# A decoder layer on one core: the conditioning matrix read in a first third and then by slices inside the token chunks

## The chip, the cores and the metric

The kernel runs on one core of a Trainium2 chip. The metric is the device time of one launch in microseconds, the median of several runs; lower is better.

## The reference, cut to what matters

One layer works on 2048 prompt tokens and 64 sample tokens (8 sequences of 8). A conditioning vector per sequence (one for the prompt, eight for the samples, so nine rows) is multiplied by a matrix of 1024 x 6144 and gives six modulation vectors of 1024 each:

```python
mod = c @ w_ada + b_ada
sh1, sc1, g1, sh2, sc2, g2 = jnp.split(mod, 6, axis=-1)
u = x * (1.0 + sc1[:, None]) + sh1[:, None]
proj = u @ w_in
...
mix = jnp.concatenate([y_pool, y_lru], axis=-1) @ w_out
x = _layer_norm(ALPHA * x + (1.0 + g1[:, None]) * mix, ln1_g, ln1_b)
u2 = x * (1.0 + sc2[:, None]) + sh2[:, None]
y_moe = _hier_moe(u2, w_group, b_group, w_route, b_route, w_gate, w_up, w_down)
x = _layer_norm(ALPHA * x + (1.0 + g2[:, None]) * y_moe, ln2_g, ln2_b)
```

Only the first third of `mod` (sh1 and sc1) is needed before the projection `proj`. The other four vectors are first used after the output projection `mix`. Between them stand the two mixers: a pooling mixer with windows of 2, 4, 8 and 16 tokens, and a recurrence with a four-tap convolution, two gates and a scan along the tokens. All numbers are 32-bit floats.

## The kernel before, in words

Each engine has its program written out by hand, in order, and waits on counting semaphores; nothing reorders it. The constants KD = 8 (blocks of 128 rows of a 1024-row matrix), NG = 4 (blocks of 128 channels of a mixer) and NCH = 8 (chunks of C = 256 prompt tokens) count the loops.

The start. SyncE (SP) issues all loads: the conditioning rows, three pieces of the matrix w_ada (each 1024 x 512, 2 MiB), small vectors, states, sample rows, then w_in in four parts of 1.5 MiB, and between these the nine other pieces of w_ada (L296 to L317), each when TensorE (PE) is done with the buffer it goes to. PE multiplies each piece by the turned conditioning rows `cT`, eight products of 128 x 512 per piece (L1463). VectorE (DVE) adds the bias (L985), adds 1 where a scale or a gate stands (L988, L989), and PE turns the first third into `modT`. SP stores the other two thirds to HBM (`mod_d`, L328). PE then turns the states and the sample rows, multiplies the modulated sample rows by w_in (24 products, L1554), and the sample tokens go through both mixers as chunk 0. ScalarE (ACT) and GpSimd (POOL) meanwhile split w_in into a high and a low part, with DVE.

The chunks. A chunk of 256 tokens is `mixers(i)` on PE: twelve column blocks ("orders" 0 to 11) of the projection, each of 24 products, which `project` writes to two PSUM banks in turn, with the gates' products ahead of orders 8 and 9 and the pooling products behind orders 9 to 11; then `turn_chunk(i + 1)` turns the next tokens. Orders 0 to 3 feed the convolution, 4 to 7 the pooling, 8 to 11 the recurrence's output gate. On DVE a trip of the loop, `chunk(i)`, is: the four pooling groups of chunk i, the guard, the low part of the next chunk's turned tokens (`u_low(i + 1)`), the recurrence of groups 0 to 2 of chunk i, the convolution of chunk i + 1 (`conv_chunk(i + 1)`, which needs orders 0 to 3 of that chunk), and the recurrence of group 3 of chunk i. So a trip on DVE ends in the middle of the next chunk on PE.

Behind the chunks. SP loads w_out in eight blocks (L355), the first four after the store of chunk 7's output, the rest after 17 small stores of sample states; ACT splits w_out (L726) when all eight are there.

Of the kernel before, what the change touches and what calls it, by code (L numbers as in the profile page):

```python
# [5 lines left out]
P = 128  # L6
# [78 lines left out]
def build(nc, A):  # L85
    with ExitStack() as ctx:
# [38 lines left out]
        def part_at(off, *shape):  # L125
# [27 lines left out]
        w_ada = [place(ada_arena, 10240 + n * 4096, KD, 512) for n in range(3)]  # L153
        mod = place(ada_arena, 22528, 6 * D)
# [55 lines left out]
        cT = sb("cT", [P, KD, NM])  # L210
# [36 lines left out]
            consts c_in vec_in ba_in gates_in gates_zero wpool_in st_in x_loaded xs_loaded w_in_in ada0 ada1 ada2  # L247
            cT_mm cT_ok ada_mm ada_ok mod_ok modT_mm modT_ok vec_mm vec_ok st_mm xsT_mm mod_stored dve_order act_order
# [9 lines left out]

        block = ctx.enter_context(nc.Block())
# [3 lines left out]
        ada_d = A["w_ada"][0].rearrange("(k p) (g n) -> g p k n", p=P, n=512)  # L263
# [30 lines left out]
        def _(sp):  # L294

            sp.dma_start(c_rows[0:1, :], A["c_prompt"]).then_inc(S["c_in"], 16)  # L296
            sp.dma_start(c_rows[1:NM, :], A["c_sample"]).then_inc(S["c_in"], 16)
            for n in range(3):
                sp.dma_start(w_ada[n], ada_d[n]).then_inc(S[f"ada{n}"], 16)
            sp.dma_start(mod[0:NM, :], all_parts(A["b_ada"][0], NM)).then_inc(S["ba_in"], 16)  # L300
            for r, name in enumerate(("b_conv", "b_a", "b_x", "lru_lambda", "pool_scale")):
                sp.dma_start(row_v[r:r + 1, :], A[name]).then_inc(S["vec_in"], 16)
            sp.dma_start(row_v[V_WCONV:NV, :], A["w_conv"][0]).then_inc(S["vec_in"], 16)
            sp.dma_start(row_a[0:DEC_B * PB, :], A["state_pool"][0].rearrange("b t c -> (b t) c")).then_inc(S["st_in"], 16)
            sp.dma_start(row_b[0:DEC_B * CB, :], A["state_conv"][0].rearrange("b t c -> (b t) c")).then_inc(S["st_in"], 16)
            sp.dma_start(row_c[0:DEC_B, :], A["state_lru"][0]).then_inc(S["st_in"], 16)
# [4 lines left out]
            sp.dma_start(w_in[:, 0:2, :], w_in_d[:, 0:2, :]).then_inc(S["w_in_in"], 16)  # L311
            with sp.Fori(1, 4) as j:
                sp.wait_ge(S["w_in_in"], 16 * j)
                sp.dma_start(w_in[:, ds(2 * j, 2), :], w_in_d[:, ds(2 * j, 2), :]).then_inc(S["w_in_in"], 16)
                for n in range(3):
                    sp.wait_ge(S["ada_mm"], 3 * j + n - 2)
                    sp.dma_start(w_ada[n], ada_d[ds(3 * j + n, 1)].rearrange("a p k n -> p (a k) n")).then_inc(S[f"ada{n}"], 16)  # L317
            sp.dma_start(xin, xp_d[0]).then_inc(S["x_loaded"], 16)
            sp.wait_ge(S["gates_zero"], 1)
# [7 lines left out]
            sp.wait_ge(S["mod_ok"], 1)  # L327
            sp.dma_start(mod_d[:, 2 * D:6 * D], mod[0:NM, 2 * D:6 * D]).then_inc(S["mod_stored"], 16)  # L328
# [15 lines left out]
            sp.wait_ge(S["ylru_ready"], NG)  # L344
            sp.dma_start(yT_d[NT - 1][:, :, 0:NS], yT[:, :, 0:NS]).then_inc(S["y_stored"], 16)
            with sp.Fori(1, NCH) as i:
                load_x(i + 1)
                store_y(i)

# [7 lines left out]
            sp.wait_ge(S["out_evac"], 3)  # L357
            load_out((2, 3, 4, 7))
# [10 lines left out]
            def load_rows():  # L369

                sp.wait_ge(S["wout_lo_dve"], KD - OUT_POOL)
                sp.wait_ge(S["mod_stored"], 16)
# [133 lines left out]
        def _(pool):  # L506
# [25 lines left out]
            for k in range(KD // 2):  # L532
                pool.wait_ge(S["win_hi"], k + 1)
                pool.wait_ge(S["ada_mm"], 10 + min(k, 1))
                pool.tensor_tensor(w_in_lo[:, k, :], w_in[:, k, :], w_in_hi[:, k, :].bitcast(F32),
                                   ALU.subtract).then_inc(S["win_lo_pool"], 1)
# [137 lines left out]
        def _(act):  # L674
            o = Order(act, S["act_order"])

            act.wait_ge(S["vec_ok"], 1)
# [4 lines left out]
            for k in range(KD):  # L682
                act.wait_ge(S["w_in_in"], 16 * (k // 2 + 1))
                if k == 6:
                    act.wait_ge(S["ada_mm"], 10)
                act.activation(w_in_hi[:, k, :], w_in[:, k, :], ACT.Copy).then_inc(S["win_hi"], 1)
# [262 lines left out]
        def _(dve):  # L949
            o = Order(dve, S["dve_order"])  # L950

            dve.wait_ge(S["cT_mm"], 1)
            dve.tensor_copy(cT[:], bank[6][:, 0:KD * NM].rearrange("p (k r) -> p k r", r=NM)).then_inc(S["cT_ok"], 1)
# [26 lines left out]
            dve.wait_ge(S["ba_in"], 16)  # L980
            with dve.Fori(0, 4) as j:
                for n in range(3):
                    dve.wait_ge(S["ada_mm"], 3 * j + n + 1)
                    cols = mod[0:NM, ds(1536 * j + 512 * n, 512)]
                    dve.tensor_tensor(cols, bank[n][0:NM, :], cols, ALU.add).then_inc(S["ada_ok"], 1)  # L985
            dve.wait_ge(S["ada_ok"], 12)

            o.step(dve.tensor_scalar(mod[0:NM, SC1:SH2], mod[0:NM, SC1:SH2], 1.0, None, ALU.add))  # L988
            dve.tensor_scalar(mod[0:NM, SC2:6 * D], mod[0:NM, SC2:6 * D], 1.0, None, ALU.add).then_inc(S["mod_ok"], 1)  # L989
# [790 lines left out]
```

## Time and profile before

| what | us |
|---|---|
| median of 3 runs | 1458.19 |
| lowest and highest run | 1457.39, 1458.48 |
| the profiled execution, first to last instruction (span) | 1455.0 |
| the profiled execution's own time | not in the profile apart from its span |
| PE busy | 1251.6 (86%) |
| DVE busy | 890.4 (61%) |
| ACT busy | 516.9 (36%) |
| POOL busy | 419.3 (29%) |

The mean granted clock of TensorE is 0.924 of its full 2.4 GHz. Busy time of PE counts pipelined products, so a busy PE isn't PE at its peak. The median of the runs lies 3.2 us above the span. The slices of the page show the DMA engines busy in the first hundred microseconds and nearly idle during the chunks, which take PE from 158.7 us to 514 us.

### The profile page before, as it was taken

To read this page: it belongs to the slowest core of one execution; us is meant where nothing else is said; L and a number is where in the kernel's file an instruction comes from. 1 tells how busy PE (TensorE), PEld (TensorE's weight loads), DVE (VectorE), ACT (ScalarE), POOL (GpSimd) and SP (SyncE) were. 2 spreads that over 40 slices of the span, in tenths; PEclk is the share of its full clock that TensorE was granted. 3 is DMA by queue.
4 is the path that set the end of the run, shared out by engine and by line. 5 is a ranking of instruction groups with operands and counts; after the bars stand their busy time and mean duration, and the time that the engine had idled before them with its cause. 6 is when DMAs were issued, how large, how long until landed. Compare 5 with 4: busy or idle time off the path is not lost.

```text
span 1455.0 us, 23155 instructions
## 1 busy us (share of the span) xinstructions
PE 1251.6 (86%) x6575; PEld 975.4 (67%) x6576; DVE 890.4 (61%) x1751; ACT 516.9 (36%) x907; POOL 419.3 (29%) x438
## 2 busy tenths in 40 slices
PE   6798899999998955999997169999999999985664
PEld 1113899999997944888885048888888888872221
DVE  2013868998988676556555845456664654224886
ACT  1100455544455331222221134445544534222331
POOL 1030122221122245565653311111111111106882
PEclk9898899999999977999997569999999999996896
DMA  8970101110111253343443266757867683316883
GB/s 276 387 272 4 37 1 58 58 58 3 54 58 58 93 190 126 132 153 139 159 133 113 79 231 221 263 210 257 278 229 238 241 277 115 115 77 235 293 291 113
DMA packets 112334, 230.17 MB, mean 158 GB/s; under 512 B 11381, under 2 KB 61049, under 8 KB 112277
## 3 DMA queue, kind: packets, MB, share of 16 engines
q1 hardware_dynamic: 93711, 162.15, 33.3%
q0 software_dynamic: 11680, 42.47, 8.5%
q10 hardware_dynamic: 6912, 25.17, 4.3%
q8 instruction: 15, 0.25, 0.1%
q14 instruction: 16, 0.13, 0.0%
HBM read 169.62 MB, written 60.27 MB: 158 GB/s over the span
## 4 chain that ended last, share of the span: by engine, by line
PE 69%; DVE 16%; DMA 4%; issue 4%; ACT 4%; SPq 2%; POOL 1%; POOLq 0%; DVEq 0%; ACTq 0%
PE bank L1489 18%; PE bank L1491 17%; PE bank L1490 17%; PE bank L1436 6%; PE bank L1463 4%; DVE arena L1400 2%; PE bank L1554 2%; DVE st L1165 1%; DVE arena L1159 1%; PE bank L1510 1%; DVE arena L1409 1%; PE bank L1624 1%; DMA arena<-in_w_in 1%; DVE parts L1092 1%; PE bank L1740 1%
## 5 line engine op out<-in xcount | busy, mean ns | idle before, releaser
L1489 PE MATMUL bank<-parts 128*128 128x256 f32 (+2 forms) x1616 | 569.1, 352 | 25.3 <-POOL parts L571 17.6
L1491 PE MATMUL bank<-parts 128*128 128x256 f32 (+2 forms) x1616 | 552.6, 342 | 0.0
L1490 PE MATMUL bank<-parts 128*128 128x256 f32 (+2 forms) x1616 | 552.0, 342 | 0.0
L1489 PEld LDWEIGHTS bank<-parts 128*128 128x128 f32 x1616 | 308.6, 191 | 63.4 <-POOL parts L571 18.0
L1491 PEld LDWEIGHTS bank<-parts 128*128 128x128 f32 x1616 | 308.1, 191 | 35.8
L1490 PEld LDWEIGHTS bank<-parts 128*128 128x128 f32 x1616 | 309.0, 191 | 31.9
L1436 PE MATMUL bank<-ident,arena 128*128 128x128 f32 (+4 forms) x788 | 118.0, 282 | 26.3 <-DMA arena<-u_d,tok_now 10.4
L1436 PEld LDWEIGHTS bank<-ident,arena 128*128 128x128 f32 (+4 forms) x788 | 94.7, 146 | 53.5 <-issue 15.8
L1740 PE MATMUL bank<-arena 128*128 128x512 f32 (+1 forms) x136 | 80.3, 748 | 50.9 <-ACT arena L925 39.6
L1331 DVE TENSOR_TENSOR parts<-arena,parts x90 | 104.9, 1221 | 17.9 <-ACT parts L859 14.2
L620 POOL COPY tok_now<-tok_i 128x1 int32 (+1 forms) x48 | 9.4, 195 | 364.7 <-PE bank L1436 347.9
L1343 DVE TENSOR_TENSOR arena<-arena,bank 128x256 f32<-128x256 f32 x48 | 20.2, 421 | 142.7 <-ACT arena L869 142.0
L549 POOL TENSOR_TENSOR arena<-arena 128x256 f32<-128x256 f32 (+1 forms) x36 | 26.1, 728 | 270.1 <-DVE h_last L1098 247.3
L1463 PE MATMUL bank<-ada_arena,cT 128*9 128x512 f32 x192 | 85.6, 608 | 16.2 <-DMA ada_arena<-in_w_ada 16.2
L1740 PEld LDWEIGHTS bank<-arena 128*128 128x128 f32 (+1 forms) x136 | 30.3, 233 | 99.6 <-issue 62.8
L859 ACT ACTIVATE parts<-arena x90 | 88.7, 1052 | 0.2 <-issue 0.2
L869 ACT ACTIVATE arena<-bank 128x256 f32<-128x256 f32 x48 | 18.5, 385 | 178.7 <-PE bank L1491 178.7
L707 ACT ACTIVATE arena<-bank,proj_b 128x256 f32<-128x256 f32 x64 | 30.4, 475 | 142.0 <-PE bank L1491 142.0
L1155 DVE TENSOR_TENSOR arena<-bank,arena 128x512 f32<-128x512 f32 (+1 forms) x34 | 21.8, 684 | 84.7 <-PE bank L1491 84.7
L1463 PEld LDWEIGHTS bank<-ada_arena,cT 128*9 128x9 f32 x192 | 17.5, 93 | 82.5 <-issue 82.5
L589 POOL TENSOR_TENSOR arena<-arena 128x1024 f32<-128x1024 f32 (+1 forms) x17 | 56.4, 3318 | 55.4 <-ACT arena L808 55.4
L1338 DVE TENSOR_TENSOR parts<-bank,parts 128x512 fp32r<-128x512 f32 x96 | 61.9, 686 | 16.6 <-ACT parts L864 16.5
(226 smaller groups left out, 1640.4 us busy)
## 6 DMA issues: line engine op xcount, KB each, us to landing
ada_arena<-in_w_ada SPq DMA_DIRECT2D x12, 2048.0 KB, 11.4
ys_d<-arena ACTq DMA_DIRECT2D x48, 512.0 KB
arena<-in_w_gate SPq DMA_DIRECT2D x16, 1024.0 KB, 6.1
arena<-in_w_up SPq DMA_DIRECT2D x16, 1024.0 KB, 9.8
arena<-in_w_down SPq DMA_DIRECT2D x16, 1024.0 KB, 14.1
arena<-in_x_prompt SPq DMA_DIRECT2D x8, 1024.0 KB, 6.7
yT_d<-arena SPq DMA_DIRECT2D x16, 512.0 KB, 4.4
arena<-yT_d SPq DMA_DIRECT2D x16, 512.0 KB, 4.8
```

Of the source, the lines that this page charges most:

```text
L589: o.step(pool.tensor_tensor(x1[b][0:n, :], z[b][0:n, :], row_tiles[0:n, 1, :], ALU.mult))
L707: act.activation(dst, bank[2 + m % 2][:, 0:C], ACT.Identity, bias=proj_b[:, m:m + 1]).then_inc(S["proj_evac"], 1)
L859: act.activation(part(w_hi, e & 1, n), raw_part(e & 1, n), ACT.Copy).then_inc(S["w_hi"], 1)
L1331: dve.tensor_tensor(part(w_lo, e & 1, n), raw_part(e & 1, n), part(w_hi, e & 1, n).bitcast(F32), ALU.subtract).then_inc(S["w_lo"], 1)
L1338: dve.tensor_tensor(xT_lo[:, k, :], bank[h][:, :].rearrange("p (k n) -> p k n", n=P), xT_hi[:, k, :].bitcast(F32), ALU.subtract).then_inc( ...
L1400: dve.scalar_tensor_tensor(z2[b][0:n, :], xo[b][0:n, :], ALPHA, z2[b][0:n, :], ALU.mult, ALU.add).then_inc(S["comb_used"], 1)
L1436: return pe.transpose(out, in_, ident[0:rows, 0:rows])
L1463: last = pe.matmul(bank[n][0:NM, :], cT[:, k, :], w_ada[n][:, k, :], start=k == 0, stop=k == KD - 1)
L1489: pe.matmul(out, x_hi, w_hi, start=start, stop=False)
L1490: pe.matmul(out, x_hi, w_lo, start=False, stop=False)
L1491: return pe.matmul(out, x_lo, w_hi, start=False, stop=stop)
L1740: last = pe.matmul(bank[2 * b + h][0:n, :], dg[b][0:n, k, 0:n], rows[0:n, 512 * h:512 * h + 512], start=k == 0, stop=k == 1)
```

## The change

Of w_ada only the first 2048 columns are read and multiplied ahead: eight loads of 1 MiB, one for each block of 128 rows, and for each block four products whose outputs go to PSUM partitions 0, 32, 64 and 96 of one bank. The other 4096 columns go by blocks of 128 rows as well: block 0 after the sample rows' projection, block k = 1 to 7 in chunk k, in two halves ("slices") of 2048 columns, four products each, ahead of orders 4 and 5. DVE adds each slice to a sum in SBUF (`mod_out`); it picks the chunk's columns of `cT` into `cT_now` at the head of its trip. The bias of these columns is added in chunk 8, and eight stores bring the sum to `mod_d` ahead of the loads of w_out. The small loads go to ACT's queue. The products of the sample rows with w_in run block by block, each behind its part of the load.

```diff
-        w_ada = [place(ada_arena, 10240 + n * 4096, KD, 512) for n in range(3)]
-        mod = place(ada_arena, 22528, 6 * D)
+        w_ada = [place(ada_arena, 12288 + k * 2048, 2048) for k in range(KD)]
+        w_ada0 = place(ada_arena, 24576, 2, 2048)
+        w_ada_next = [at(2048, 2048), at(5184, 2048)]
+        mod_in = at(3072, 512)
+        mod_out = at(8768, 2, 512)
+        b_out = at(2048, 2, 512)
...
+            for k in range(KD):
+                sp.dma_start(w_ada[k], ada_d[k][:, 0:2048]).then_inc(ada_in[k], 16)
             sp.dma_start(xs[0:NS, :], xs_d).then_inc(S["xs_loaded"], 16)
+            for j in range(4):
+                sp.dma_start(w_in[:, 2 * j:2 * j + 2, :], w_in_d[:, 2 * j:2 * j + 2, :]).then_inc(S[f"w_in{j}"], 16)
+            sp.wait_ge(S["cT_mm"], 1)
             sp.dma_start(xin, xp_d[0]).then_inc(S["x_loaded"], 16)
+            sp.wait_ge(S["ada_mm"], KD)
+            sp.dma_start(w_ada0, ada_d[0][:, 2048:6144].rearrange("p (b n) -> p b n", b=2)).then_inc(S["ada0_in"], 16)
...
+            sp.wait_ge(S["prj_copied"], 1)
+            load_slice(1, 0)
+            load_slice(1, 1)
             sp.dma_start(yT_d[NT - 1][:, :, 0:NS], yT[:, :, 0:NS]).then_inc(S["y_stored"], 16)
-            with sp.Fori(1, NCH) as i:
+            with sp.Fori(1, NCH - 1) as i:
                 load_x(i + 1)
+                for b in range(2):
+                    sp.wait_ge(S["slice_mm"], 2 * i + 1 + b)
+                    load_slice(i + 1, b)
                 store_y(i)
+            load_x(NCH)
...
+            store_y(NCH - 1)
+            sp.wait_ge(S["slice_ok"], 2 * KD + 1)
+            for b in range(2):
+                for j in range(4):
+                    cols = slice(2048 * b + 512 * j + 2048, 2048 * b + 512 * j + 2560)
+                    sp.dma_start(mod_d[:, cols], mod_out[32 * j:32 * j + NM, b, :]).then_inc(S["mod_stored"], 16)
...
             sp.wait_ge(S["out_evac"], 3)
+            sp.wait_ge(S["mod_stored"], 16 * 8)
             load_out((2, 3, 4, 7))
...
+            def add_slice(n, b, src):
+
+                dve.wait_ge(S["slice_ok"], n)
+                dve.wait_ge(S["slice_mm"], n + 1)
+                dve.tensor_tensor(mod_out[:, b, :], src[:, :], mod_out[:, b, :], ALU.add).then_inc(S["slice_ok"], 1)
...
+            dve.wait_ge(S["slice_mm"], 2)
+            o.did(dve.tensor_scalar(mod_out[0:64, 0, :], bank[1][0:64, :], 1.0, None, ALU.add))
+            o.step(dve.tensor_copy(mod_out[64:P, 0, :], bank[1][64:P, :]))
+            dve.tensor_scalar(mod_out[:, 1, :], bank[0][:, :], 1.0, None, ALU.add).then_inc(S["slice_ok"], 2)
...
             def chunk(i, last=False):
 
+                if not last:
+                    dve.wait_ge(S["slice_ok"], 2 * i)
+                    dve.tensor_copy(cT_now[:], cT[:, ds(i, 1), :].rearrange("p a r -> p (a r)")).then_inc(S["cT_picked"], 1)
+                if last:
+                    dve.wait_ge(S["bias_in"], 16 * 8)
+                    dve.wait_ge(S["slice_ok"], 2 * KD)
+                    dve.tensor_tensor(mod_out, mod_out, b_out, ALU.add).then_inc(S["slice_ok"], 1)
+                for b in range(0 if last else 2):
+                    add_slice(2 * i + b, b, bank[4 + b])
                 for g, w in enumerate(WINDOWS):
...
+            for k in range(KD):
+                if k == 4:
+                    turn_vectors()
+                pe.wait_ge(ada_in[k], 16)
+                for j in range(4):
+                    last = pe.matmul(bank[0][32 * j:32 * j + 32, :], cT[:, k, :], w_ada[k][:, 512 * j:512 * j + 512],
+                                     start=k == 0, stop=k == KD - 1)
+                last.then_inc(S["ada_mm"], 1)
+
+            def ada_slice(c, w, out):
+
+                for j in range(4):
+                    last = pe.matmul(out[32 * j:32 * j + 32, :], c, w[:, 512 * j:512 * j + 512], start=True, stop=True)
+                last.then_inc(S["slice_mm"], 1)
...
-            def mixers(i, turn_next):
+            def mixers(i, turn_next, slices=False):
                 for order in range(3 * NG):
+                    if slices and order in (4, 5):
+                        b = order - 4
+                        pe.wait_ge(S["gates_evac"], 2 * NG * i)
+                        pe.wait_ge(S["cT_picked"], i)
+                        pe.wait_ge(S[f"ada_in{b}"], 16 * i)
+                        ada_slice(cT_now[:], w_ada_next[b], bank[4 + b])
+                    if slices and order == 2 * NG:
+                        pe.wait_ge(S["slice_ok"], 2 * i + 2)
```

On PE, in the loop over chunks, between order 3 and order 5 (the L1523 to L1525 products are those of `project`, in the numbering of the changed kernel; L1503 is `ada_slice`):

```order
L1525 MATMUL bank<-parts 128x256
L1561 REGISTER_ALU
L1563 REGISTER_ALU [waits cT_picked,gates_evac]
L1503 MATMUL bank<-arena,cT_now 32x512 [waits ada_in0]
L1503 MATMUL bank<-arena,cT_now 32x512 x3
L1571 REGISTER_ALU
L1523 MATMUL bank<-parts 128x256 [waits proj_evac]
```

Before, the products of order 4 followed those of order 3 with only the wait on `proj_evac` between; now a wait on `cT_picked` and four slice products stand ahead of them, and everything behind is queued behind that wait.

On DVE, at the head of a trip of the loop over chunks, the kernel before (the L1063 copy is the last of `conv_chunk(1)`, L1073 the first pooling sum):

```order
L1063 COPY arena<-arena 128x3 [waits xc_ready]
L1142 UNCONDITIONAL_BRANCH
L1142 ISA
L1073 TENSOR_TENSOR arena<-arena 128x256 [waits proj_evac]
L68 ISA
```

and the changed kernel at the same place:

```order
L1092 COPY arena<-arena 128x3 [waits xc_ready]
L1180 UNCONDITIONAL_BRANCH
L1180 ISA
L1097 ISA [waits slice_ok]
L1097 COPY cT_now<-cT 128x32
L1018 REGISTER_ALU [waits slice_ok]
L1019 TENSOR_TENSOR arena<-bank,arena 128x512 [waits slice_mm]
L1018 REGISTER_ALU [waits slice_ok]
L1019 TENSOR_TENSOR arena<-bank,arena 128x512 [waits slice_mm]
L1106 ISA
L1111 TENSOR_TENSOR arena<-arena 128x256 [waits proj_evac]
```

The copy into `cT_now` is the trip's first instruction, behind the whole of the trip before, and two sums that wait for the slices now stand ahead of the pooling.

On SP, behind the chunks, the changed kernel (L331 stores chunk 7's output, L363 the modulation, L370 loads w_out):

```order
L331 DMA yT_d<-arena 1024x1x128 [waits ylru_ready,pool_evac]
L331 DMA yT_d<-arena 1024x1x128
L363 DMA mod_d<-arena 9x512 [waits slice_ok]
L363 DMA mod_d<-arena 9x512 x7
L370 DMA arena<-in_w_out 128x1024 [waits mod_stored,out_evac]
L370 DMA arena<-in_w_out 128x1024 x3
```

Before, the first load of w_out followed the store directly; now eight stores and the wait for their landing stand between.

## Rows read from the trace of the kernel before

**Rows 1.** Page, chain of work that ended last: shares of the span by engine

```profile
PE 69%; DVE 16%; DMA 4%; issue 4%; ACT 4%; SPq 2%; POOL 1%; POOLq 0%; DVEq 0%; ACTq 0%
```

**Rows 2.** Windows: stretch, length, busy by engine (instructions), clock, DMA share, GB/s

```profile
60.00:80.00 20.00, 20.00 (x48) 4.22 (x47) 1.44 (x4) 1.76 (x2) 0.00 (x0) 1.00 1.03 386
```

**Rows 3.** Timeline of PE, the start: start, us, line, operation [idle before <- releaser]

```profile
9.72 15.30 PE L1463 MATMUL bank<-ada_arena,cT 128*9 128x512 f32 x32 [4.97 <-DMA ada_arena<-in_w_ada]
...
44.03 63.28 PE L1463 MATMUL bank<-ada_arena,cT 128*9 128x512 f32 x144 [11.22 <-DMA ada_arena<-in_w_ada]
113.14 1.87 PE L1436 MATMUL bank<-ident,ada_arena 9*128 9x9 f32 x16 [5.83 <-DVE ada_arena L989]
...
120.72 23.02 PE L1554 MATMUL bank<-arena 128*65 128x512 f32 x48 [1.86 <-DVE arena L1007]
...
155.17 3.69 PE L1436 MATMUL bank<-ident,arena 128*128 128x128 f32 x16
158.68 0.58 PE L1489 MATMUL bank<-parts 128*128 128x256 f32 x1
```

**Rows 4.** Timeline of DVE, the start

```profile
107.46 0.68 DVE L985 TENSOR_TENSOR ada_arena<-bank,ada_arena 9x512 f32 x1 [6.19 <-PE bank L1463]
108.17 3.67 DVE L988 TENSOR_SCALAR ada_arena<-ada_arena 9x2048 f32<-9x2048 f32 x1
...
145.06 0.11 DVE L1021 MEMSET arena<- 128x60 f32 x1 [17.82 <-PE bank L1436]
```

**Rows 5.** Timeline of SP's queue, the start: issues of loads

```profile
0.82 0.35 SPq L296 DMA_DIRECT2D arena<-in_c_prompt  x1
...
1.57 4.46 SPq L299 DMA_DIRECT2D ada_arena<-in_w_ada  x3
```

**Rows 6.** Chain of work in order of time: first product of chunks 2 and 3

```profile
202.65 0.38 PE bank L1489
...
246.25 0.38 PE bank L1489
```

**Rows 7.** Timeline of ACT: evacuation of order 3 in chunks 1 and 2

```profile
170.78 0.47 ACT L707 ACTIVATE arena<-bank,proj_b 128x256 f32<-128x256 f32 x1 [2.33 <-PE bank L1491]
...
214.45 0.47 ACT L707 ACTIVATE arena<-bank,proj_b 128x256 f32<-128x256 f32 x1 [2.33 <-PE bank L1491]
```

**Rows 8.** Timeline of DVE: chunk 1's first pooling sum; the recurrence during chunk 2

```profile
179.61 0.43 DVE L1073 TENSOR_TENSOR arena<-arena 128x256 f32<-128x256 f32 x1
...
204.70 0.29 DVE L1051 TENSOR_SCALAR arena<-arena 128x256 f32<-128x256 f32 x1 [1.20 <-ACT arena L747]
...
225.82 0.28 DVE L1051 TENSOR_SCALAR arena<-arena 128x256 f32<-128x256 f32 x1
...
229.83 0.15 DVE L1098 COPY h_last<-arena 128x1 f32<-128x1 f32 x1
```

**Rows 9.** Source line L1463: count, ns min/median/max, first and last start

```profile
L1463 PE MATMUL bank<-ada_arena,cT x192: 592/592/1061, 9.7 to 106.7; 128*9 128x512 f32 x192
```

**Rows 10.** Timeline of PE at its restart behind the chunks

```profile
531.69 0.79 PE L1489 MATMUL bank<-parts 128*128 128x512 f32 x1 [17.56 <-POOL parts L571]
```

**Rows 11.** Windows there (columns as in Rows 2)

```profile
532.00:534.00 2.00, 2.00 (x6) 1.52 (x6) 2.00 (x2) 0.00 (x0) 2.00 (x1) 0.50 0.10 37
534.00:536.00 2.00, 2.00 (x9) 1.59 (x8) 1.97 (x2) 0.00 (x0) 1.00 (x1) 0.79 0.83 277
```

**Rows 12.** Timeline of SP's queue behind the chunks

```profile
495.04 3.53 SPq L355 DMA_DIRECT2D arena<-in_w_out  x4
...
504.06 0.28 SPq L362 DMA_DIRECT2D result<-arena  x1
504.38 0.28 SPq L363 DMA_DIRECT2D result<-arena  x1
508.64 1.79 SPq L355 DMA_DIRECT2D arena<-in_w_out  x4
```

**Rows 13.** Timeline of ACT behind the chunks: the split of w_out

```profile
516.92 7.68 ACT L726 ACTIVATE parts<-arena 128x1024 fp32r<-128x1024 f32 x8 [2.27 <-DMA arena<-in_w_out]
```

More of the change, by code:

```diff
@@ L209, in build @@
         ones = sb("ones", [P, P])
[L210 removed]
+        cT = sb("cT", [P, KD, 32])
+        cT_now = sb("cT_now", [P, 32])
         modT = sb("modT", [P, 2 * KD, NM])
@@ L257, in build @@
             fsd_ready fnorm fg_ok fo_ok os0 os1""".split()}
+        ada_in = [sem(f"ada_k{k}") for k in range(KD)]
         block = ctx.enter_context(nc.Block())
@@ L1451, in _ @@
             pe.wait_ge(S["cT_ok"], 1)
-            def ada(j, first=False):
-                for n in range(3):
-                    if first and n == 2:
-                        turn_vectors()
-                    pe.wait_ge(S[f"ada{n}"], 16 * (j + 1))
-                    if not first:
-                        pe.wait_ge(S["ada_ok"], 3 * j + n - 2)
-                    for k in range(KD):
-                        last = pe.matmul(bank[n][0:NM, :], cT[:, k, :], w_ada[n][:, k, :], start=k == 0, stop=k == KD - 1)
-                    last.then_inc(S["ada_mm"], 1)
-            ada(0, first=True)
-            with pe.Fori(1, 4) as j:
-                ada(j)
+            for k in range(KD):
+                if k == 4:
+                    turn_vectors()
+                pe.wait_ge(ada_in[k], 16)
+                for j in range(4):
+                    last = pe.matmul(bank[0][32 * j:32 * j + 32, :], cT[:, k, :], w_ada[k][:, 512 * j:512 * j + 512],
+                                     start=k == 0, stop=k == KD - 1)
+                last.then_inc(S["ada_mm"], 1)
+            def ada_slice(c, w, out):
+                for j in range(4):
+                    last = pe.matmul(out[32 * j:32 * j + 32, :], c, w[:, 512 * j:512 * j + 512], start=True, stop=True)
+                last.then_inc(S["slice_mm"], 1)
             pe.wait_ge(S["mod_ok"], 1)
-            for k in range(2 * KD):
-                last = turn(bank[6][:, k * NM:(k + 1) * NM], mod[0:NM, k * P:(k + 1) * P], NM)
+            for i in range(4):
+                last = turn(bank[6][:, i * P:(i + 1) * P], mod_in[:, i * P:(i + 1) * P], P)
             last.then_inc(S["modT_mm"], 1)
@@ L1550, in _ @@
             pe.wait_ge(S["uTs_ready"], 1)
-            for n in range(3):
-                cols = slice(DH, 2 * DH) if n == 0 else slice(0, DH) if n == 1 else slice(2 * DH, 3 * DH)
-                for k in range(KD):
+            for k in range(KD):
+                if k % 2 == 0:
+                    pe.wait_ge(S[f"w_in{k // 2}"], 16)
+                for n in range(3):
+                    cols = slice(DH, 2 * DH) if n == 0 else slice(0, DH) if n == 1 else slice(2 * DH, 3 * DH)
                     last = pe.matmul(bank[2 + n][0:NS + 1, :], uTs[:, k, :], w_in[:, k, cols], start=k == 0, stop=k == KD - 1)
-                last.then_inc(S["rows_mm"], 1)
+                    if k == KD - 1:
+                        last.then_inc(S["rows_mm"], 1)
             for n in range(3):
```

84 lines of the change are left out of this document (38 added, 46 removed).

## The prediction, made before the changed kernel ran

> **What bounds the kernel now.** The chain of work that ended last comes first: 69% of the span is PE [rows 1], so a change is worth what it does to PE's own sequence, stage by stage. Two stages matter here. In the start, the timeline of PE shows what it does until the first chunk's first product at 158.68 us: the products with w_ada begin at 9.72 and, after an 11.22 us wait for a load, run from 44.03 for 63.28 us [rows 3]. In the windows the loads move 386 GB/s meanwhile [rows 2], so this stage is bound by loads and PE together, and nothing of chunk 1 can go on beside it. In the chunks PE is the bound, at 246.25 - 202.65 = 43.60 us per chunk [rows 6], and DVE lags behind it: the timeline of DVE is what the reader has to hold against PE's.
>
> **The start, part by part.** A product with a 512-column piece costs 63.28 / 72 = 0.88 us, since each leaves two records [rows 3, 9].
>
> Loads: of w_ada 8 MiB instead of 24 come first. The first 2 MiB took from 1.57 to 9.72 [rows 3, 5]; at 386 GB/s that is 5.4 us of moving and 2.7 of lead. With SP's first issue at 0.82 [rows 5], 1 MiB every 2.7 us lands its first part at 6.2 and its last at 0.8 + 2.7 + 8 x 2.7 = 25.2.
>
> What four products into four partition strips cost (one slice, s) no row shows. Bounds: four one after another, 4 x 0.88 = 3.52; all at once, 0.88. Each product is two records, and the second reuses the first one's strip; if only neighbours overlap, the four take five half-products, 5 x 0.44 = **2.2 us**. I take that, which is also the middle. The Trainium skill, "TensorE: Matmul & The Clock Gate", Part 3, says that products with outputs at different 32-partition strips run concurrently, with 2.38 times the speed for three, and that they start and end in order. By 2.38 the four would take some 1.5 us (an estimate from that page), and the sum below would be some 12 us lower; no run here shows it.
>
> Last product: 25.2 + 2.2 = 27.4. Then one sum of 0.68 [rows 4] in place of the 5.7 us from 107.46 to 113.14 [rows 3, 4]: 28.3 with handoffs. From 113.14 to 120.72 takes 7.58, of which 1.87 are 16 small turns; four turns of 128x128 take 3.69 / 4 = 0.92 instead [rows 3]: 34.9. The 24 sample products take 23.02 [rows 3]: 57.9. Their loads (6.5 MB behind 25.2, so 42) are there in time by blocks. From 143.74 to 158.68 is 14.94 [rows 3], which stays, and ahead of the stage that DVE begins at 145.06 [rows 4] now stand two slices (4.4) and three sums of 0.68: 6.4. Chunk 1 starts at 57.9 + 14.9 + 6.4 = **79.2, a gain of 79.5**. With s = 0.88 the gain is 83.4; with 3.52 PE and not the loads sets the first part (6.2 + 8 x 3.52 = 34.4) and it is 70.
>
> The small loads on ACT's queue I cost at nothing: the first product's piece lands at 6.2, and ACT has nothing to do before w_in. If the conditioning rows came late behind the big loads, each microsecond would show one for one.
>
> **The chunks.** PE now waits at order 4 for DVE to pick the columns, which DVE does at the head of its trip [the order listings]. Where does that head lie? In chunk 2, PE starts at 202.65 [rows 6] and is done with order 3 when ACT evacuates it, 214.45 [rows 7]. DVE starts the recurrence at 204.70 and ends group 3 at 229.98 [rows 8]; between, its timeline has no gap of note, so it is behind with work, not waiting. With 0.2 us for the copy the pick comes at 230.2: PE **waits 15.7 us** in the middle of every chunk. In chunk 1 the head is at 179.61 [rows 8] and order 3 done at 170.78 [rows 7]: 9.0 us. This cannot be worked off in later chunks: the recurrence starts only after the chunk's boundary (it waits for ACT's roots [rows 8]), so the pick lies as far behind the chunk's start each time. Sum over chunks 1 to 7: 9.0 + 6 x 15.7 = **103 us**.
>
> What is queued behind the wait: orders 4 to 11, the turn of the next tokens, the next chunk. DVE's pooling starts later, too, but is needed only behind order 9; the sums of the slices (0.68 each) fall in DVE's new idle time.
>
> The clock: after 17.56 us of idle PE restarted [rows 10] at the lower level (1.2 of 2.4 GHz), 0.50 granted, and at 0.79 in the next two microseconds [rows 11]. That loses 2.3 x 0.5 + 2 x 0.21 = 1.6 us per restart, seven times 11.
>
> The slices themselves: 14 x 2.2 = 31 us on PE, on the path (14 x 0.88 = 12 to 14 x 3.52 = 49). Their loads hide: 2 MiB per chunk need 5.4 us at 386 GB/s, in chunks in which the queues are nearly idle, and are issued a chunk ahead.
>
> **Behind the chunks.** The loads of w_out stood at 495.04 [rows 12] and end on the path: ACT waited 2.27 us for them [rows 13]. Ahead of them now stand eight stores, one per 0.32 us as the small stores from 504.06 to 504.38, and their landing, 4.0 us as from 504.66 to 508.64 [rows 12]: 6.6 us later, all on the path.
>
> **The sum.** -79.5 + 103 + 11 + 31 + 6.6 = **+72**. The profiled execution, 1455.0 us of span, becomes 1527; the median of the runs lies 3.2 above that span, and I add the same: **1531 us**.
>
> **The rivals.**
> *The four strips in turn.* Against overlap speaks that no two records of before overlap by more than the pipelining does; for it, that the strips are separate. With s = 3.52: -70 + 103 + 11 + 49 + 6.6 = +100, 1558 us.
> *The four strips all at once.* s = 0.88: -83.4 + 103 + 11 + 12 + 6.6 = +50, 1508 us. Every product being two records on one strip speaks against it.
> *The pick is early, and it gets faster.* If DVE reached its head before PE reached order 4, neither wait nor restart would be: -79.5 + 31 + 6.6 = -42, 1416 us. The point that decides is 42 / 7 = 6.0 us of wait and restart per chunk. Against it: order 3 is evacuated at 214.92 [rows 7], and the recurrence of group 3 alone takes from 225.82 to 229.98 behind it [rows 8], so even if all else on DVE cost nothing, the wait would be 4.8 us with the copy, and 6.4 with the restart.
> *The change does not do what it says* has no room here: the wait stands in the order listing.
>
> **How the numbers follow.** My forecast (strips overlap by neighbours) has 0.52, with a range of its own of 1518 to 1542 from the clock in the start (the sample products took 23.02 / 24 = 0.96 us against 0.88) and the landing of the stores (0 to 9 us). In turn: 0.26. All at once: 0.18. The early pick: 0.03, all of it faster; 0.01 for none of these, near no change. The range, 1502 to 1562, takes in the three slow cases with their bounds. A change under 0.2% (2.9 us) cannot be told from none. Slower by more than that has 0.96, faster 0.03, within it 0.01.
>
> **What would show it.** In the profile of the changed kernel: the first chunk starts near 79 us; PE's idle time ahead of `ada_slice` (released by DVE's copy into `cT_now`) is the largest wait of PE, near 103 us in seven waits, six near 15.7; four slice products end about 2.2 us after they start (0.9 or 3.5 for the rivals); the granted clock falls to its lower level at each of these waits; chunks 2 to 7 take some 65 us each; w_out lands some 6 us later against the end of chunk 8. It is wrong if DVE's copy stands ahead of order 4's turn, or if chunks take under 50 us.

## The result, and the profile after

The changed kernel takes **1526.6 us** (median of 4 runs, 1524.5 to 1527.54); the kernel before took 1457.79 on the same chip (4 runs, 1456.68 to 1458.48). The ratio is 1.0474, with an interval of 1.046 to 1.0489: slower by 69 us. The forecast was 1531. The profiled execution took 1526.17 us with a span of 1524.4, at a mean granted clock of 0.891 (0.924 before).

The page of the changed kernel, shares of the chain that ended last by engine [rows 1], and the row of the slice products in its list of groups (busy, mean ns, idle before and its releaser):

```profile
PE 58%; DVE 25%; ACT 5%; issue 5%; DMA 4%; SPq 1%; POOL 1%; DVEq 0%; POOLq 0%; ACTq 0%
...
L1503 PE MATMUL bank<-arena,cT_now 128*32 128x512 f32 x112 | 21.0, 833 | 108.9 <-DVE cT_now L1097 108.9
```

PE's share of the chain fell from 69 to 58% and DVE's rose from 16 to 25%. The 56 products of the slices (112 records) are busy for 21 us, the lower clock of the first slice behind each wait included, and PE idles 108.9 us ahead of them. The view of what PE waited for (us in total, times, longest) gives the count:

```profile
PE bank L1503 <- DVE cT_now L1097: 108.9, 7, 16.7
```

The timeline of PE, from the last part of the first third of w_ada to the second chunk's first slice [rows 3], and the first product of chunk 8:

```profile
29.18 1.06 PE L1496 MATMUL bank<-ada_arena,cT 128*32 128x512 f32 x8 [2.30 <-DMA ada_arena<-in_w_ada]
31.13 4.77 PE L1474 MATMUL bank<-ident,arena 128*128 128x128 f32 x24 [0.89 <-DVE arena L1010]
42.54 23.10 PE L1598 MATMUL bank<-arena 128*65 128x512 f32 x48 [6.64 <-DVE arena L1035]
...
66.72 1.92 PE L1503 MATMUL bank<-ada_arena,cT 128*32 128x512 f32 x16
...
84.39 0.53 PE L1523 MATMUL bank<-parts 128*128 128x256 f32 x1
...
105.69 1.94 PE L1503 MATMUL bank<-arena,cT_now 128*32 128x512 f32 x8 [9.39 <-DVE cT_now L1097]
112.59 1.06 PE L1503 MATMUL bank<-arena,cT_now 128*32 128x512 f32 x8
171.32 1.94 PE L1503 MATMUL bank<-arena,cT_now 128*32 128x512 f32 x8 [16.69 <-DVE cT_now L1097]
...
539.86 0.58 PE L1523 MATMUL bank<-parts 128*128 128x256 f32 x1 [0.68 <-ACT arena L807]
```

In the kernel before, chunk 8's first product stands at

```profile
471.38 0.58 PE L1489 MATMUL bank<-parts 128*128 128x256 f32 x1 [0.68 <-ACT arena L782]
```

Chunk 1 starts at 84.39 in place of 158.68. In chunk 1 PE waits 9.39 us for the pick, in chunk 2 16.69, and the first slice behind each wait takes 1.94 where a later one takes 1.06. On DVE the pick of chunk 2 stands directly behind the recurrence of chunk 1's last group (timeline of DVE):

```profile
169.23 0.75 DVE L1135 TENSOR_TENSOR_SCAN arena<-arena,h_last 128x256 f32<-128x256 f32 x1
170.02 0.15 DVE L1136 COPY h_last<-arena 128x1 f32<-128x1 f32 x1
170.87 0.22 DVE L1097 COPY cT_now<-cT 128x32 f32 x1 [0.70 <-DVE h_last L1136]
```

The kernel before has a gap like it between two trips, behind the last row of [rows 8]:

```profile
230.56 0.60 DVE L1073 TENSOR_TENSOR arena<-arena 128x256 f32<-128x256 f32 x1 [0.57 <-DVE h_last L1098]
```

The windows behind the first and the last of the seven waits (columns as in [rows 2]) show the granted clock as the last figure but two:

```profile
104.00:106.00 2.00, 0.31 (x4) 0.21 (x8) 1.23 (x4) 0.00 (x0) 0.00 (x0) 0.50 0.94 334
106.00:108.00 2.00, 2.00 (x10) 0.44 (x3) 0.31 (x1) 0.00 (x0) 0.00 (x0) 0.50 1.14 370
108.00:110.00 2.00, 2.00 (x11) 2.00 (x11) 0.38 (x1) 0.00 (x0) 0.00 (x0) 0.50 1.08 389
110.00:112.00 2.00, 2.00 (x12) 2.00 (x11) 0.00 (x0) 0.00 (x0) 0.00 (x0) 0.50 0.93 385
112.00:114.00 2.00, 2.00 (x16) 1.03 (x16) 0.28 (x1) 0.47 (x1) 0.00 (x0) 0.99 0.08 33
...
498.00:500.00 2.00, 2.00 (x11) 1.58 (x8) 0.69 (x1) 0.00 (x0) 0.00 (x0) 0.50 0.96 285
500.00:502.00 2.00, 2.00 (x15) 2.00 (x14) 0.00 (x0) 0.00 (x0) 0.00 (x0) 0.71 0.95 246
```

Behind the first restart (105.69) the lower level lasts 6.3 us, behind the last (496.55) 4.6, where the kernel before had 3.1 at its restart [rows 11]. PE is busy throughout and the lower level is half of the full one, so I put the loss at half of that time (an estimate; the first slice at 1.94 beside 1.06 shows the size).

Behind the chunks, the timeline of SP's queue [rows 12]:

```profile
561.88 1.28 SPq L331 DMA_DIRECT2D yT_d<-arena  x2
563.20 4.85 SPq L363 DMA_DIRECT2D mod_d<-arena  x8
569.31 1.78 SPq L370 DMA_DIRECT2D arena<-in_w_out  x4
...
581.11 1.79 SPq L370 DMA_DIRECT2D arena<-in_w_out  x4
```

and that of ACT at its split of w_out [rows 13]:

```profile
588.67 7.68 ACT L751 ACTIVATE parts<-arena 128x1024 fp32r<-128x1024 f32 x8 [5.44 <-DMA arena<-in_w_out]
```

ACT's wait for w_out is 5.44 us in place of 2.27. The whole difference of the two spans, cut at PE's first product of chunk 1 and of chunk 8 and at ACT's split:

| stretch | before | after | difference |
|---|---|---|---|
| to chunk 1's first product | 158.7 | 84.4 | -74.3 |
| chunks 1 to 7 | 312.7 | 455.5 | +142.8 |
| chunk 8 to ACT's split of w_out | 45.5 | 48.8 | +3.3 |
| from there to the end of the span | 938.1 | 935.7 | -2.4 |

### The profile page after: what moved, and what is told of

Read it like the earlier page. It is cut to its first block, busy times and chain, and to the rows that moved or that the text cites. A ratio compares the mean times of both kernels' runs of the same rounds, so it can differ in the third digit from the quotient of the medians.

```text
span 1524.4 us, 23171 instructions
## 1 busy us (share of the span) xinstructions
PE 1215.3 (80%) x6563; PEld 973.2 (64%) x6564; DVE 882.3 (58%) x1765; ACT 517.3 (34%) x907; POOL 420.5 (28%) x438
## 4 chain that ended last, share of the span: by engine, by line
PE 58%; DVE 25%; ACT 5%; issue 5%; DMA 4%; SPq 1%; POOL 1%; DVEq 0%; POOLq 0%; ACTq 0%
PE bank L1523 16%; PE bank L1525 15%; PE bank L1524 15%; PE bank L1474 5%; DVE arena L1081 4%; DVE arena L1067 3%; DVE arena L1438 2%; ACT parts L717 2%; DMA ada_arena<-in_w_ada 2%; PE bank L1598 2%; PE bank L1503 1%; DVE arena L1135 1%; DVE arena L1197 1%; DVE st L1203 1%; PE bank L1544 1%
## 5 line engine op out<-in xcount | busy, mean ns | idle before, releaser
L1523 PE MATMUL bank<-parts 128*128 128x256 f32 (+2 forms) x1616 | 575.3, 356 | 29.3 <-POOL parts L587 20.6
L1525 PE MATMUL bank<-parts 128*128 128x256 f32 (+2 forms) x1616 | 556.1, 344 | 0.0
L1523 PEld LDWEIGHTS bank<-parts 128*128 128x128 f32 x1616 | 313.2, 194 | 84.7 <-POOL parts L587 21.0
L1525 PEld LDWEIGHTS bank<-parts 128*128 128x128 f32 x1616 | 312.3, 193 | 35.7
L1524 PEld LDWEIGHTS bank<-parts 128*128 128x128 f32 x1616 | 313.5, 194 | 31.8
L1474 PE MATMUL bank<-ident,arena 128*128 128x128 f32 (+3 forms) x792 | 119.0, 283 | 29.4 <-DMA arena<-u_d,tok_now 10.3
L1474 PEld LDWEIGHTS bank<-ident,arena 128*128 128x128 f32 (+3 forms) x792 | 95.7, 147 | 58.3 <-issue 23.5
L1503 PE MATMUL bank<-arena,cT_now 128*32 128x512 f32 x112 | 21.0, 833 | 108.9 <-DVE cT_now L1097 108.9
L1503 PEld LDWEIGHTS bank<-arena,cT_now 128*32 128x32 f32 x112 | 2.5, 124 | 111.3 <-issue 110.3
L557 POOL TENSOR_TENSOR uI<-arena 128x256 f32<-128x256 f32 (+1 forms) x36 | 24.9, 691 | 176.5 <-ACT arena L762 173.0
L605 POOL TENSOR_TENSOR arena<-arena 128x1024 f32<-128x1024 f32 (+1 forms) x17 | 56.6, 3328 | 55.4 <-ACT arena L833 55.4
```

The lines of the kernel that those rows point to most:

```text
L605: o.step(pool.tensor_tensor(x1[b][0:n, :], z[b][0:n, :], row_tiles[0:n, 1, :], ALU.mult))
L1474: return pe.transpose(out, in_, ident[0:rows, 0:rows])
L1503: last = pe.matmul(out[32 * j:32 * j + 32, :], c, w[:, 512 * j:512 * j + 512], start=True, stop=True)
L1523: pe.matmul(out, x_hi, w_hi, start=start, stop=False)
L1524: pe.matmul(out, x_hi, w_lo, start=False, stop=False)
L1525: return pe.matmul(out, x_lo, w_hi, start=False, stop=stop)
```

## The experiments

Each run is one execution with its profile; only the last one has four. The runs without slices, with order 4 first and the first two with the pick early ran on one chip, on which the kernel before took 1460.1 us (one run); "one strip", "POOL late" and "all together" on another, on which it took 1455.2 (median of 7). Whole times compared across the two are loose by some microseconds. The table has what the sections below read: when chunk 1's first product starts, how long it is from there to chunk 8's first product, and how long from there to the end of the span. "Own time" is that of the profiled execution.

| run | own time | chunk 1 starts | chunks 1 to 7 | behind |
|---|---|---|---|---|
| before (of the result above) | 1457.8 (median) | 158.7 | 312.7 | 983.6 |
| after | 1526.2 | 84.4 | 455.5 | 984.5 |
| no slices in the chunks | 1384.6 | 84.3 | 313.5 | 985.0 |
| order 4 ahead of the slices | 1527.0 | 85.5 | 451.8 | 987.9 |
| pick early | 1456.3 | 84.4 | 376.2 | 994.0 |
| pick early, banks 6 and 7 | 1420.0 | 85.0 | 339.2 | 994.1 |
| the same, one strip | 1474.9 | 84.8 | 374.5 | 1013.8 |
| banks 6 and 7, POOL late | 1410.5 | 79.95 | 338.9 | 989.9 |
| all together, slices later | 1396.9 | 80.9 | 329.8 | 984.5 |

### The start alone: no slices in the chunks

```
-                mixers(i, lambda: turn_chunk(i + 1), slices=True)
+                mixers(i, lambda: turn_chunk(i + 1))
...
-                    dve.tensor_copy(cT_now[:], cT[:, ds(i, 1), :]...).then_inc(S["cT_picked"], 1)
...
-                    add_slice(2 * i + b, b, bank[4 + b])
...
-            load_slice(1, 0)
-            load_slice(1, 1)
...
-                    load_slice(i + 1, b)
```

> Edit: the start as changed, but in chunks 1 to 7 no pick, no slice product, no load of a slice and no sum: the last four modulation vectors lack the parts of seven of the eight row blocks of w_ada. Theory (the start gains 74 us, the tail loses 3, and all the rest of the loss is in the slices of the chunks): 1457.8 - 74.3 + 3.3 - 2.4 = 1384 us, chunks 2 to 7 at 43.6 us each. Rival (the shorter start is given back in the chunks in another way than by slices and waits): over 1395 us.

Measured: 1384.61 us, and chunk 8's first product on PE's timeline at

```profile
397.82 0.58 PE L1513 MATMUL bank<-parts 128*128 128x256 f32 x1 [0.67 <-ACT arena L802]
```

so chunks 1 to 7 take 313.5 us, as before the change (312.7). What is gained in the start is kept. Nearly all of the loss lies in what was put into the chunks; the tail ahead of w_out adds the 3.3 of the table above.

### The pick early

```
-                if not last:
-                    dve.wait_ge(S["slice_ok"], 2 * i)
-                    dve.tensor_copy(cT_now[:], cT[:, ds(i, 1), :]...).then_inc(S["cT_picked"], 1)
...
                     add_slice(2 * i + b, b, bank[4 + b])
+                if not last:
+                    dve.tensor_copy(cT_now[:], cT[:, ds(i + 1, 1), :]...).then_inc(S["cT_picked"], 1)
```

A copy of the same form, ahead of the loop, picks chunk 1's columns.

> Edit: DVE copies the columns for chunk 1 before the loop and those for chunk i+1 right behind the two sums of chunk i; all else as in the changed kernel (own time 1526.2 us in its profiled execution). Theory (PE's wait for the pick and the restart behind it are the cost): the seven waits, 108.9 us, and their restarts, about 22 us, vanish. A smaller wait takes their place, since PE must wait ahead of order 8 for the sums, which still stand at the head of DVE's trip, about 29 us behind the chunk's start, while PE would be at order 8 after about 25: some 4 us in chunks 2 to 7, 24 us, with the restarts behind it up to 42. 1526 - 109 - 22 + 24 to 42 = 1419 to 1437 us. Rival (the slices, their loads and the sums are the cost, and the wait only shows where they are paid): the same time is lost at other places, over 1500 us.

Measured: 1456.3 us beside 1460.1 for the kernel before on that chip, and 70 below the changed one. The seven waits for the pick are gone. What PE waits for in the chunks instead:

```profile
PE bank L1544 <- DVE arena L1019: 23.5, 6, 4.1
PE bank L1503 <- DMA arena<-in_w_ada: 7.6, 1, 7.6
```

The first line is the wait ahead of order 8 for the sums, as expected, 23.5 us; with the restarts behind it, it costs 37.0 (376.2 against the 339.2 of the next run, which lacks it). The second was not expected: the first two slices are loaded only when the sample stage ends, and in the changed kernel the wait for the pick had hidden them. I had taken the time of the load as free because "their loads hide", which holds for chunks 2 to 7 alone. Behind the chunks this run is 9.5 us longer than the changed one; that is taken up below. The rival, which had the slices themselves as the cost, is out for the bulk: their products and loads are all still there. 1456 lies 19 above the top of the expected 1419 to 1437, by this load with its restart (about 10, from the next run) and the 9.5 behind the chunks.

### The pick early, and banks 6 and 7

```
-                        ada_slice(cT_now[:], w_ada_next[b], bank[4 + b])
-                    if slices and order == 2 * NG:
-                        pe.wait_ge(S["slice_ok"], 2 * i + 2)
+                        ada_slice(cT_now[:], w_ada_next[b], bank[6 + b])
...
                     project(i, column(order), order, C, KD * (i - 1) if order == 0 else None)
+                    if slices and order == 2 * NG + 1:
+                        pe.wait_ge(S["slice_ok"], 2 * i + 2)
```

> Edit: the early pick, and the slices go to banks 6 and 7 (used next by the pooling products behind order 9) in place of 4 and 5; the wait for the sums moves from order 8 to order 9. Theory (waits at orders 4 and 8 are the whole loss of the chunks): no wait of PE for cT_now or for the sums over 1 us is left; DVE's two sums (1.4 us) may make the pooling products 1.5 us late per chunk: 1526 - 109 - 22 = 1395 to 1407 us. Rival (DVE is then the bound of the chunks, since it lags behind PE by more than half a chunk): PE waits for the pooling input instead, over 3 us per chunk, over 1420 us.

Measured: 1420.02 us. The wait ahead of order 8 is gone, none for the pooling input takes its place, and chunks 1 to 7 take 339.2 us. Against the run without slices that is 25.7 more. By ACT's first copy in each chunk, chunk 1 takes 55.9 us and the chunks behind it 46.1, so about 10 go to the load in chunk 1 (a wait of 7.8 us) with its restart. The other chunks take 2.2 more than the 43.9 of the run without slices, and two slices at 1.06 are 2.1 of that. DVE, for all its lag, was not the bound of the chunks. The time is 13 above the top of what was expected, by the load in chunk 1 and 9.5 behind the chunks.

What happens there shows in the stage of the layer norm. POOL's timeline in one pass of it:

```profile
577.93 2.41 POOL L605 TENSOR_TENSOR arena<-arena 128x1024 f32<-128x1024 f32 x1 [4.91 <-ACT arena L833]
```

DVE's at the same time:

```profile
576.90 1.23 DVE L1219 TENSOR_TENSOR arena<-arena 128x1024 f32<-128x1024 f32 x1 [0.42 <-issue]
578.17 3.25 DVE L1220 TENSOR_TENSOR arena<-arena 128x1024 f32<-128x1024 f32 x1
```

and PE's next step:

```profile
581.55 1.09 PE L1474 MATMUL bank<-ident,arena 128*128 128x128 f32 x8 [3.04 <-DVE arena L1220]
```

DVE's sum L1220 begins 0.24 us behind POOL's L605 and takes 3.25 us, where L1219 of the same shape took 1.23 just before it: POOL is done at 580.34, and DVE 1.08 us later. It looks as if DVE stood still until POOL was done. PE waits 3.04 us for it. In the changed kernel DVE's L1220 takes 1.35 us in the mean over this stage, here 1.72. The same sum parts all nine kernels: its mean is 1.35 in the five with 983.6 to 987.9 us behind the chunks and 1.72 in the four with 989.9 and more. PE's waits for it grow from 9.0 us in the changed kernel to 15.9 here, 7 of the 9.5; where the rest goes is open. What seems to set it is how the three engines stand to each other when the loop is entered, since the code of this stage is the same in all these kernels; that was read from the traces and not tried by itself.

### POOL late: two engines and one operand path

The start had the same picture. DVE's timeline of the changed kernel:

```profile
36.13 2.44 DVE L1032 COPY arena<-modT 128x8 f32<-128x8 f32 x1
...
38.48 0.68 DVE L1033 TENSOR_TENSOR arena<-bank,modT 128x512 f32<-128x512 f32 x1
39.20 3.29 DVE L1035 TENSOR_TENSOR arena<-arena,modT 128x512 f32<-128x512 f32 x1
```

and POOL's, four operations in one row:

```profile
35.09 15.60 POOL L551 TENSOR_TENSOR parts<-arena,parts 128x1536 fp32r<-128x1536 f32 x4 [30.56 <-ACT parts L711]
```

The edit, on top of the run with banks 6 and 7:

```
+            pool.wait_ge(S["uTs_ready"], 1)
             for k in range(KD // 2):
                 pool.wait_ge(S["win_hi"], k + 1)
```

> Edit: the run with banks 6 and 7, and POOL begins its four low parts of w_in only when DVE has written the sample tokens (L1035). Theory (DVE's copy L1032, 2.44 us for 128x8, and its sum L1035, 3.29 us, are held up by POOL's first operation of 3.9 us beside them, and take 0.17 and 0.69 as before when POOL is quiet): 2.3 + 2.6 = 4.9 us less ahead of chunk 1, which starts at 80.2 in place of 85.1; own time 1415 us where the run with banks 6 and 7 took 1420.0. Rival (these two are long for a reason of their own, as the shape of their operands): chunk 1 starts at 85 again. The stage behind the chunks moved by up to 9 us between the runs, so the start of chunk 1 decides, not the whole time.

Measured, the same three operations on DVE's timeline, with POOL quiet:

```profile
37.23 0.17 DVE L1033 COPY arena<-modT 128x8 f32<-128x8 f32 x1
...
37.31 0.68 DVE L1034 TENSOR_TENSOR arena<-bank,modT 128x512 f32<-128x512 f32 x1
38.02 0.69 DVE L1036 TENSOR_TENSOR arena<-arena,modT 128x512 f32<-128x512 f32 x1
```

and PE's sample products behind them:

```profile
38.77 22.43 PE L1599 MATMUL bank<-arena 128*65 128x512 f32 x48 [1.77 <-DVE arena L1036]
```

2.44 became 0.17 (in the run with banks 6 and 7 it was 2.86), 3.29 became 0.69, and chunk 1 starts at 79.95 in place of 85.02: the 4.9 us are shown. (The whole time fell by 9.5, since the stage behind the chunks came out 4.2 shorter as well.) The times of the single operations say that DVE is not slowed down but held. The copy takes 2.44, 2.86 and 1.67 us in the changed kernel and the runs with banks 6 and 7 and without slices, but it ends at 38.57, 39.37 and 39.45, each time within 0.04 us of the end of POOL's first operation (38.53, 39.34 and 39.42). The sum L1035 of the changed kernel ends 0.55 behind POOL's second one (42.49 against 41.94), which is about its own length. The middle operation, which reads one of its two inputs from a PSUM bank, took 0.68 both times. The Trainium skill, "SBUF — State Buffer", section "Who interferes with whom", says that DVE and GpSimd share a pair of SBUF ports as a lock: a DVE instruction with two SBUF inputs, or a copy in a two-port mode, and a GpSimd instruction that reads SBUF wait for each other's end. These rows agree, the untouched middle row too; which mode the copy ran in, no row shows.

### Order 4 ahead of the slices

```
-                    if slices and order in (4, 5):
-                        b = order - 4
+                    if slices and order == 4:
+                        pe.wait_ge(S["cT_picked"], i)
+                    if slices and order == 5:
+                        for b in range(2):
...
-                        pe.wait_ge(S["cT_picked"], i)
-                        pe.wait_ge(S[f"ada_in{b}"], 16 * i)
-                        ada_slice(cT_now[:], w_ada_next[b], bank[4 + b])
+                            pe.wait_ge(S[f"ada_in{b}"], 16 * i)
+                            ada_slice(cT_now[:], w_ada_next[b], bank[4 + b])
```

> Edit: the wait for the pick stays ahead of order 4, but order 4's 24 products go first behind it and both slices ahead of order 5. Theory (the slices' 32-column products, the first behind the wait, keep the granted clock at its lower level longer, 3.1 us lost per restart where 1.6 was read from the kernel before): 1526 - 7 x 1.5 = 1516 us, and the granted clock back at 1.0 within 3 to 4 us of the restart. Rival (the length at the lower level has nothing to do with which products come first): 1524 to 1528 us, the lower level for 6 us again.

Measured: 1526.96 us in place of 1526.2, no change; chunks 1 to 7 are 3.7 us shorter, which the start (1.1) and the stage behind the chunks (3.3) take back. Here the products that restart the clock are the 128-column ones. Windows behind chunk 1's restart at 106.76:

```profile
106.00:108.00 2.00, 1.24 (x6) 1.25 (x7) 0.44 (x3) 0.00 (x0) 0.00 (x0) 0.50 1.06 320
108.00:110.00 2.00, 2.00 (x11) 2.00 (x11) 0.00 (x0) 0.00 (x0) 0.00 (x0) 0.50 1.04 419
110.00:112.00 2.00, 2.00 (x19) 1.41 (x22) 0.00 (x0) 0.47 (x1) 0.00 (x0) 0.99 0.25 100
```

This first restart has the lower level for only 3.3 us, which fits the theory. The later ones, from the same view in steps of half a microsecond, do not: 4.1, 4.6, 4.9, 5.1, 5.2, 5.2 us. In the changed kernel the seven are 6.3, 5.6, 5.1, 4.9, 4.7, 4.6, 4.6. One row falls and the other rises, and they cross, though within a kernel the same products stand behind every wait. The run with the early pick bears this out: at its six waits ahead of order 8, again with the same products behind each, the lower level lasts between 3.0 and 5.9 us. So something other than the products that come first sets most of the length, and the theory falls. It may be the moment of the restart; that was not tried. The seven sum to 35.9 us in the changed kernel, of which half, 18, is put down as lost: 2.6 us per restart.

### One strip

```
-                    last = pe.matmul(out[32 * j:32 * j + 32, :], c, w[...], start=True, stop=True)
+                    rows = out[0:32, :] if one else out[32 * j:32 * j + 32, :]
+                    last = pe.matmul(rows, c, w[...], start=True, stop=True)
```

(`w[...]` stands for the same columns in both; `one` is set in the slices of chunks 1 to 7, on top of the run with banks 6 and 7)

> Edit: the run with banks 6 and 7, but the four products of a slice all go to partitions 0 to 31 of the bank, so that three of the four pieces of the last four modulation vectors lack the parts of seven row blocks. Theory (the four strips are worked on side by side, so four products take the time of one): in one strip they take four times as long, 3.5 us per slice in place of 0.95, 14 x 2.6 = 36 us more: 1456 us. Rival (the four products take 0.95 us together whatever the strips, because a product of 32 stationary columns is short): 1418 to 1422 us.

Measured, the two slices of chunk 1 on PE's timeline, the first mostly at the lower clock, the second at the full one:

```profile
104.34 5.75 PE L1504 MATMUL bank<-arena,cT_now 128*32 128x512 f32 x8 [7.73 <-DMA arena<-in_w_ada]
113.08 3.62 PE L1504 MATMUL bank<-arena,cT_now 128*32 128x512 f32 x8
```

Four products in one strip take 3.62 us, in four strips 1.06. (In one strip they also write the same rows of the bank; this run does not tell the two apart.) Chunks 1 to 7 grew by 35.3 us (339.2 to 374.5), as expected. The whole time is 54.9 longer and misses the expected 1456: 19.7 came behind the chunks. There PE has two waits of 7.0 us for an expert's weights that the run with banks 6 and 7 does not have:

```profile
PE bank L1524 <- DVE parts L1369: 14.1, 2, 7.0
```

The tokens' routing to the experts depends on the vectors that this run changes, and that may be the cause; but the run without slices changes them too and took 985.0 there, so it is not shown.

### All together

On top of the run with POOL late: the slices ahead of orders 6 and 7, ACT takes them out of the banks, DVE adds them beside its low parts, and the tail is reordered.

```
+            sp.wait_ge(S["p_free"], NG)
+            load_slice(1, 0)
...
-                    if slices and order in (4, 5):
+                    if slices and order in (6, 7):
...
+                    if not last and m in (6, 7):
+                        act.wait_ge(S["slice_mm"], 2 * i + m - 5)
+                        act.activation(sl_t[m - 6], bank[m][:, :], ACT.Copy).then_inc(S["slice_sb"], 1)
...
                     u_low(i + 1)
+                    for b in range(2):
+                        dve.tensor_tensor(mod_out[:, b, :], mod_out[:, b, :], sl_t[b], ALU.add)...
+                    dve.tensor_copy(cT_now[:], cT[:, ds(i + 1, 1), :]...).then_inc(S["cT_picked"], 1)
...
-            sp.wait_ge(S["mod_stored"], 16 * 8)
-            load_out((2, 3, 4, 7))
+            load_out((2, 3, 4))
```

> Edit: the run with POOL late, and the slices ahead of orders 6 and 7 in place of 4 and 5, ACT copies them out of banks 6 and 7 and DVE adds them behind its low parts of the next chunk's tokens; the first slice is loaded as soon as the sample rows are pooled; behind the chunks only the load of w_out's block 7 waits for the stores of the modulation, and these stand behind the loads of blocks 2 to 4. Theory: start -74.3 - 4.9, slices 7 x 1.9 = +13, tail +1, stage behind the chunks -2 to +9, no wait for a slice in chunk 1: 1457.8 - 65 to -54 = 1393 to 1404 us, chunks 2 to 7 at 45.5 us each. Rival (ACT's two copies and DVE's two sums delay the gates or the pooling by as much as they saved): chunks over 46.5 us, over 1408 us.

Measured: **1395.09 us** (4 runs, 1394.87 to 1396.89) against 1455.22 for the kernel before on this chip: ratio 0.9584, interval 0.9567 to 0.9602, faster by 60 us. The slices of chunk 1 and the first product of chunk 8 on PE's timeline:

```profile
98.81 1.07 PE L1511 MATMUL bank<-arena,cT_now 128*32 128x512 f32 x8
102.87 1.06 PE L1511 MATMUL bank<-arena,cT_now 128*32 128x512 f32 x8
...
410.73 0.58 PE L1531 MATMUL bank<-parts 128*128 128x256 f32 x1 [0.68 <-ACT arena L814]
```

No slice has a wait of note ahead of it, and the first one runs at the full clock. Chunks 1 to 7 take 329.8 us, 16.3 more than without slices: 2.3 per chunk, of which 2.1 are the products. By ACT's first copy in each, chunks 2 to 6 take 46.2 us: more than the 45.5 expected, since a chunk of the run without slices takes 43.9 and not the 43.6 of before [rows 6], and under the 46.5 of the rival. The whole time is within the range given. The edits of this run came together, so what each gave is not told apart.

## Why the prediction was right

The forecast was a slowdown of 72 us, and 69 came, by the mechanism named as the likeliest: PE waits in the middle of every chunk for a copy that DVE makes at the head of its trip. The runs with the pick early show it: with the wait gone, 70 to 106 us go with it. (The forecast's sum comes to 1530.3 and was written down as 1531.) The measured waits, restarts and slices (108.9, 18 and 14.8) add up to 141.7 of the 142.0 us by which chunks 1 to 7 of the changed kernel exceed those of the run without slices. The terms:

- **The wait, 103 us predicted, 108.9 measured.** Right, with each wait about 1 us longer than the 15.7 read from DVE's lag. The step had priced the copy at 0.2 but not the 0.70 us that DVE takes from the trip's last instruction to the next trip's first. The kernel before shows such a gap of 0.57 at the same place, so it could have been read.
- **The slices, 14 x 2.2 = 31 us predicted, about 14 x 1.06 = 15 measured.** The step that failed is "if only neighbours overlap, the four take five half-products". Four strips take 1.06 us together (one product: 0.88), where one strip took 3.62. The value lies next to the bound "all at once". Speaking against that bound from the pairs of records was wrong; the estimate of 1.5, worked out from the 2.38 for three strips in the Trainium skill ("TensorE: Matmul & The Clock Gate", Part 3), was nearer, and still too long: four strips gave 3.62 / 1.06 = 3.4 times the speed.
- **The restarts, 1.6 each and 11 in all predicted, 2.6 and 18 worked out from the measured lengths.** The step took its size from one restart [rows 11], at which the lower level lasted 3.1 us. Behind the seven it lasted 4.6 to 6.3. One restart was no measure, since the length differs from restart to restart in one kernel.
- **The start, 79.2 predicted, 84.39 measured.** The last part of w_ada was waited for until 29.18, not 25.2: "1 MiB every 2.7 us" took the speed of a stage in which hardly anything else was loaded, while now the rows on ACT's queue load beside it (the conditioning rows held PE's first instruction until 6.42); that they are the cause was not tried. With the cheaper last slice 2.8 of it is left. DVE's two operations beside POOL cost 4.9, a step that the sum did not have: moving the loads forward let POOL's split of w_in begin while DVE still prepared the sample tokens. The two slices at the stage's end cost 1.92 in place of 4.4. 2.8 + 4.9 - 2.5 = 5.2.
- **The tail, 6.6 predicted, 3.3 measured.** The stores and their landing put the first loads of w_out 569.31 - 563.20 = 6.1 us behind the store, as said. But ACT waits for the second four loads, which stand behind the small stores of the states; the issue of the first four took 1.8 us in place of 3.5, that of the small stores 6.9 in place of 6.1, and the wait behind them 2.7 in place of 4.0. So the second four were issued 41.2 us behind chunk 8's start in place of 37.3, and landed 0.7 faster. "All on the path" did not hold.
- **The rest at nothing**: -2.4 measured. That is less than the stage behind the chunks moves between the runs here; its cause is not shown.

The time was closer than its terms: a chunk was to cost 15.7 + 4.4 + 1.6 = 21.7 us more, and cost some 16.6 + 2.1 + 2.6 = 21.3. The slices were too dear by 16 us over all chunks, the waits and restarts too cheap by 13. Of the rivals, "all at once" had the right size for the slices, and its 1508 was too low by the restarts, the start and the waits. The rival of the early pick was priced at 1416 us, and the run that made the pick early without a new wait took 1420; that is partly luck too: about 10 us of it were a load and 9.5 the stage behind the chunks, which the price did not hold, while the slices came 16 cheaper.

## What to carry to other kernels

A helper copy at the head of a loop is due when the engine that makes it reaches that head, not when the engine that needs it does: hold the two timelines against each other, and put the copy in the trip before. When a wait is taken away, look at what it hid; here it was a load and a second wait, each of which cost a restart of the clock. A resource that two engines share, as DVE and POOL do, shows in a profile as one shape with two durations: the operation that is held counts as busy, and not as a wait.

## What was not expected of the hardware

- A DVE operation of 0.17 us took 2.44, and one of 0.69 took 3.29, beside a POOL operation on SBUF; with POOL held back both fell to 0.17 and 0.69, as in the kernel before. The copy ended within 0.04 us of POOL's operation in three runs, whenever it began. In the layer norm the same seems to have moved the whole time by up to 9.5 us between kernels that are alike there.
- The lower clock level lasted between 3.0 and 6.3 us behind a restart, and differed by up to 2.9 us between restarts of one kernel that had the same products behind them.
- Four fp32 products of 32 stationary columns into four strips took 1.06 us, into one strip 3.62.
